# Sums of squares of the last layer's head norms: one four-pass product against two one-pass products of a high and a low part

## The reference

```python
def rms_norm_2(x, g):
    xf = x.astype(jnp.float32)
    y = xf * lax.rsqrt(jnp.mean(xf * xf, axis=-1, keepdims=True) + EPS)
    return (y * g.astype(jnp.float32)).astype(x.dtype)

k = rms_norm_2(k.reshape(B, T, B_HEADS, HEAD_DIM), k_gain)
q = rms_norm_2((h @ w_q).reshape(B, T, B_HEADS, HEAD_DIM), q_gain)
...
decay = c[:, :, q0:q1, None] - c[:, :, None, :q1]
s = jnp.where(causal, s + decay, -jnp.inf)
p = jax.nn.softmax(s, axis=-1)
```

## Time and profile before

| what | value |
|---|---|
| runs, median of 3 (lowest to highest) | 1271.04 us (1270.38 to 1271.95) |
| the profiled execution's own time | 1271.81 us |
| its span from first to last instruction | 1269.8 us |
| mean granted TensorE clock | 0.997 |
| share of the span with an instruction: TensorE matmuls, weight loads | 98%, 92% |
| VectorE, ScalarE, GpSimd | 64%, 58%, 29% |
| instructions | 26957 |
| transfers | 218.68 MB, mean 172 GB/s |

### The profile page before, as it was taken

One profiled execution on the slowest core, in us unless ns is written; L12 is line 12 of the kernel. 1 busy time (PEld: TensorE's weight loads), 2 busy tenths in 40 slices (PEclk: granted clock), 3 DMA queues, 4 the chain that ended last, 5 costly groups with the idle time before them and its releaser, 6 DMA issues.

```text
span 1269.8 us, 26957 instructions
## 1 busy us (share of the span) xinstructions
PE 1245.5 (98%) x9610; PEld 1173.9 (92%) x9610; DVE 812.0 (64%) x1441; ACT 734.6 (58%) x1368; POOL 365.6 (29%) x413
## 2 busy tenths in 40 slices
PE   6999999999999999999999899999999999999998
PEld 6988999998998999998889599999999889999887
DVE  5687755566677655557799975554547766755554
ACT  6476766655455566666566864444346776544433
POOL 2011344421000144441133037770001210678100
PEclk9999999999999999999999899999999999999999
DMA  7542666667665466667655056556555443665764
GB/s 262 182 125 85 195 186 181 185 212 203 206 188 167 135 186 183 193 182 217 183 163 153 6 165 184 178 175 184 172 166 194 146 135 105 194 182 183 199 188 159
DMA packets 65761, 218.68 MB, mean 172 GB/s; under 512 B 9152, under 2 KB 13456, under 8 KB 65552
## 3 DMA queue, kind: packets, MB, share of 16 engines
q1 hardware_dynamic: 63344, 210.99, 54.9%
q10 hardware_dynamic: 2336, 6.58, 1.6%
HBM read 214.04 MB, written 1.08 MB: 169 GB/s over the span
## 4 chain that ended last, share of the span: by engine, by line
PE 76%; issue 10%; DVE 5%; POOL 4%; ACT 3%; DMA 1%; POOLq 0%; SPq 0%; ACTq 0%; DVEq 0%
PE bank L346 19%; PE bank L348 18%; PE bank L347 18%; PE bank L362 8%; PE bank L363 4%; POOL scratch L613 1%; DVE wlo L330 1%; POOL scratch L611 1%; PE bank L960 1%; PE bank L945 1%; POOL ahi_alo L615 1%; PE bank L942 1%; DVE scratch L601 1%; ACT ahi_alo L586 1%; ACT whi L325 1%
## 5 line engine op out<-in xcount | busy, mean ns | idle before, releaser
L330 DVE TENSOR_TENSOR wlo<-raw,whi 128x1024 fp32r<-128x1024 f32 (+1 forms) x391 | 479.7, 1228 | 150.1 <-ACT whi L325 148.3
L346 PE MATMUL bank<-uhi,whi 128*128 128x256 f32 (+1 forms) x1824 | 525.6, 288 | 11.5 <-DVE wlo L330 10.6
L348 PE MATMUL bank<-uhi,wlo 128*128 128x256 f32 (+1 forms) x1824 | 518.0, 284 | 0.0
L347 PE MATMUL bank<-ulo,whi 128*128 128x256 f32 (+1 forms) x1824 | 517.5, 284 | 0.0
L325 ACT ACTIVATE whi<-raw 128x1024 fp32r<-128x1024 f32 (+1 forms) x391 | 407.7, 1045 | 178.6 <-PE bank L363 102.8
L346 PEld LDWEIGHTS bank<-uhi,whi 128*128 128x128 f32 x1824 | 345.4, 189 | 19.8 <-issue 17.1
L348 PEld LDWEIGHTS bank<-uhi,wlo 128*128 128x128 f32 x1824 | 345.6, 189 | 0.0
L347 PEld LDWEIGHTS bank<-ulo,whi 128*128 128x128 f32 x1824 | 344.2, 189 | 0.5
L362 PE MATMUL bank<-ahi_alo,whi 128*128 128x512 f32 x608 | 212.4, 393 | 0.0
L363 PE MATMUL bank<-ahi_alo,wlo 128*128 128x256 f32 x608 | 170.5, 280 | 0.0
L346 PE MATMUL bank<-ahi_alo,whi 128*128 128x272 f32 (+1 forms) x560 | 162.6, 290 | 0.4 <-DVE wlo L330 0.4
(11 more groups left out here) (292 smaller groups left out, 1332.5 us busy)
## 6 DMA issues: line engine op xcount, KB each, us to landing
raw<-stream SPq DMA_DIRECT2D x391, 512.0 KB, 3.9
scratch<-decay ACTq DMA_DIRECT2D x8, 416.0 KB, 4.3
scratch<-relh ACTq DMA_DIRECT2D x8, 384.0 KB, 3.5
scratch<-scratch SPq DMA_DIRECT2D x60, 34.0 KB, 2.6
constants<-consts SPq DMA_DIRECT2D x1, 1300.0 KB, 11.0
h<-xT SPq DMA_DIRECT2D x4, 256.0 KB, 5.4
out<-h SPq DMA_DIRECT2D x8, 128.0 KB, 2.4
scratch<-scratch SPq DMA_DIRECT2D x16, 16.0 KB, 3.2
```

Source lines behind the costliest of these rows:

```text
L330: dve.tensor_tensor(wlo[:, s, 0:w], raw[:, s, 0:w], whi[:, s, 0:w].bitcast(F32), ALU.subtract).then_inc(w_lo, 1)
L346: pe.matmul(dst, hi, a, start=first and i == 0, stop=False)
L347: pe.matmul(dst, hi, b, start=False, stop=False)
L348: mm = pe.matmul(dst, lo, a, start=False, stop=last and i == chunks - 1)
```

## The change

The squares are kept as two parts in the one-pass type: a high part, which ScalarE's Square writes directly into the (here unused) chunks 16 and 17 of the split buffer `ahi`, and a low part, which GpSimd computes as the full square minus the high part and writes to `alo`. TensorE makes two one-pass matmuls per block, with a copy of `headones` in the one-pass type (`sums_r`, made once on ScalarE), in place of one four-pass matmul.

For odd blocks ScalarE writes the full square too, as a second Square; for even blocks GpSimd computes it as a product. The stat of the even block moves from between the scores and unit(2s+1) to inside that unit, after five of its eight chunks. GpSimd's additions for pair s+1 come behind the low parts of blocks 2s and 2s+1. VectorE's evictions wait for the low part instead of the Square before they reuse a buffer.

```diff
--- before.py
+++ after.py
@@ -305,6 +305,7 @@
         ki_copied, wi_scaled, wi_turned, wi_done, ix_ready, ix_relu, ix_acc, ix_mask, ix_clear = sems(
             "ki_copied wi_scaled wi_turned wi_done ix_ready ix_relu ix_acc ix_mask ix_clear")
         h_half = sem("h_half")
+        fox_sq_k, fox_sq_q, fox_lo = sems("fox_sq_k fox_sq_q fox_lo")
         f_exp, f_log = sems("f_exp f_log")
         q_tables, q_neg, q_eps = sems("q_tables q_neg q_eps")
         t_q, t_gather, t_s, t_row, t_max, t_exp, t_p, t_pt, t_pts, t_o, t_ohi, t_olo = sems(
@@ -1164,6 +1165,35 @@
             return j if j < 2 else j + 1
 
         FOX_V = {5: 2, 6: 17, 7: 18}
+        sums_r = ahi[:, 20, 0:P]
+
+        def fox_square(j):
+            return (x[:, 16 + j % 2, fox_cols(j)] for x in (ahi, alo))
+
+        def fox_low_pool(pool, j):
+
+            cols, i, r0 = fox_cols(j), fox_at(j), RFIRST["fkq"]
+            hi, lo = fox_square(j)
+            if j % 2:
+                pool.wait_ge(fox_sq_q, j // 2 + 1)
+            else:
+                y = yb[:, i % 4, cols]
+                pool.wait_ge(evac, BSTART["fkq"] + i + 1)
+                pool.tensor_tensor(ysq[:, 0, cols], y, y, ALU.mult).then_inc(fox_sq_k, 1)
+                pool.wait_ge(fox_sq_k, j // 2 + 1)
+            pool.wait_ge(y_sq, r0 + j + 1)
+            pool.tensor_tensor(lo, ysq[:, j % 2, cols], hi.bitcast(F32), ALU.subtract).then_inc(fox_lo, 1)
+
+        def fox_pool(pool):
+            for j in (0, 1):
+                fox_low_pool(pool, j)
+            for s in (0, 1):
+                decay_pool(pool, s)
+            for s in range(1, fox.pairs):
+                for j in (2 * s, 2 * s + 1):
+                    fox_low_pool(pool, j)
+                if s + 1 < fox.pairs:
+                    decay_pool(pool, s + 1)
 
         def fox_pe(pe):
             a, n0, b0, r0, v0, last = fox, START["fkq"], BSTART["fkq"], RFIRST["fkq"], VFIRST["fv"], fox.pairs - 1
@@ -1190,9 +1220,11 @@
 
             def stat(j):
                 cols = fox_cols(j)
-                pe.wait_ge(y_sq, r0 + j + 1)
-                pe.matmul(block_bank(fox_at(j))[:, 0:width(cols)], const("headones"), ysq[:, j % 2, cols],
-                          start=True, stop=True).then_inc(y_stat, 1)
+                pe.wait_ge(fox_lo, j + 1)
+                hi, lo = fox_square(j)
+                dst = block_bank(fox_at(j))[:, 0:width(cols)]
+                pe.matmul(dst, sums_r, hi, start=True, stop=False)
+                pe.matmul(dst, sums_r, lo, start=False, stop=True).then_inc(y_stat, 1)
 
             def last_early_turn():
                 v = LATE["fv"] - 1
@@ -1228,8 +1260,7 @@
                 else:
                     late_turn(5)
                 scores(s - 1)
-                stat(2 * s)
-                unit(2 * s + 1)
+                unit(2 * s + 1, inside=lambda s=s: stat(2 * s))
                 if s >= 2:
                     values(s - 2)
             values_unit(6, 2 * last + 1, inside=lambda: stat(2 * last + 1))
@@ -1256,7 +1287,14 @@
                 cols, i = fox_cols(j), fox_at(j)
                 act.wait_ge(evac, b0 + i + 1)
                 act.wait_ge(y_stat, r0 + j - 1)
-                act.activation(ysq[:, j % 2, cols], yb[:, i % 4, cols], ACT.Square).then_inc(y_sq, 1)
+                if j == 0:
+                    act.activation(sums_r, const("headones"), ACT.Copy).then_inc(link.sem, 1)
+                    act.wait_ge(link.sem, link.next())
+                act.activation(ahi[:, 16 + j % 2, cols], yb[:, i % 4, cols], ACT.Square).then_inc(y_sq, 1)
+                if j % 2:
+                    if j > 1:
+                        act.wait_ge(fox_lo, j - 1)
+                    act.activation(ysq[:, 1, cols], yb[:, i % 4, cols], ACT.Square).then_inc(fox_sq_q, 1)
 
             def rms(j):
                 cols = fox_cols(j)
@@ -1330,7 +1368,7 @@
                 cols, i = fox_cols(j), fox_at(j)
                 dve.wait_ge(w_used, n0 + i + 1)
                 if j >= 3:
-                    dve.wait_ge(y_sq, r0 + j - 3 if j > 4 else r0 + 2)
+                    dve.wait_ge(fox_lo, j - 3 if j > 4 else 2)
                 if j in (2, 5):
                     dve.wait_ge(v_turned, VFIRST["fv"] + (5 if j == 2 else 6))
                 dve.tensor_tensor(yb[:, i % 4, cols], bank[2 + (b0 + i) % 2][:, 0:width(cols)], rstd[:, 0, cols],
@@ -2552,8 +2590,7 @@
             pool.memset(area(V0, 8 * 384).rearrange("p (c n) -> p c n", n=384)[:, :, 256:384], 0.0).then_inc(v_cleared, 1)
             sqrelu_pool(pool, "up2", WHOLE, 2 * FC1, 0)
             norm_pool(pool, 6, WHOLE)
-            for s in range(fox.pairs):
-                decay_pool(pool, s)
+            fox_pool(pool)
             norm_pool(pool, 7, FIRST)
             sqrelu_pool(pool, "up3", FIRST, 2 * FC1 + FC2, FC2)
```

## The result

| | before | after |
|---|---|---|
| median of 5 runs (lowest to highest) | 1271.04 us (1270.18 to 1272.27) | 1277.87 us (1276.91 to 1279.15) |
| ratio, 95% interval | | 1.0051 (1.0039 to 1.0063) |
| the profiled execution's own time, its span | 1271.81, 1269.8 us | 1279.15, 1277.2 us |
| mean granted TensorE clock | 0.997 | 0.997 |

The change costs 6.8 us (5.0 to 8.0 by the interval). 1277.7 was predicted, inside 1273.6 to 1281.5.

A forecast was written before the change was run, and what follows sets the result against it. A ScalarE and VectorE chain was taken as the bound from the third pair: start +2.65, six rounds of 11.33 instead of 10.59 make +7.1, less 0.2 twice, +6.7. On the median 1277.7 us, range 1273.6 to 1281.5.

The forecast's parts named there:

- The round closes through ScalarE and VectorE, with TensorE in it nowhere: One pair of heads, 10.59 us between odd stats: a ScalarE and VectorE chain bounds it from the third pair on.
- X: End of VectorE's even (key) block eviction in a round; E+3.74 before, predicted E+4.48.
- Cheaper sum product: Two one-pass matmuls per stat save TensorE 0.16 to 0.2 us; only Ln's earlier start, 0.60 instead of 0.80, counts.
- E: End of VectorE's odd (query) block eviction, from which times in a round are counted; next one predicted at X+6.85.
- The second path: ScalarE's second Square delays the weight split 0.33 us; low split ends E+2.98, before the stat path's E+3.22, adding nothing.
- Port collision: GpSimd's additions slow VectorE's low split and norm product through shared SBUF ports; 0.10 us a round reaches X.
- leg T: Not in the prediction: way from odd stat through TensorE's scores, VectorE's maximum and softmax Exp to the next E.
- The start: First blocks, before steady rounds: low parts wait behind GpSimd's eight additions and a low split; stat 3 late by 2.65 us.
- TensorE is the bound: Rival: the odd stat is covered and TensorE's savings count; -4.5, 1266.5 us; chance 0.07.
- the full collision: Rival: the odd subtract waits out VectorE's low split, 1.2 us in each of six rounds; 1285 us; chance 0.12, partial included.
- Only the split path counts: Rival: only the held-back weight split costs, 0.33 us a round; 1274 us, or 1273 with start covered; chance 0.18 together.
- Rival 4: Additions spill past X, removing the even stat's 0.7 us cover; up to 0.5 us a round, 1280.5; 0.63 with forecast.

The follow-up runs named there:

- before_reorder: Kernel before the change, with VectorE evicting the even block before making the attention output's low part; 1270.39 us, 0.9993, and 0.9988 when timed again.
- after_reorder: Changed kernel, with VectorE evicting the even block before making the attention output's low part; 1277.89 us, 1.0057 against the kernel before.
- decay_later: Changed kernel, with GpSimd's causal additions moved behind the next even block's low part; 1277.05 us, 1.0044 against the kernel before.
- square_twice: Changed kernel, with odd blocks back on the four-pass product, plus a second ScalarE Square that nobody reads; 1274.49 us, 1.0027 against the kernel before.
- odd_vector: Changed kernel, with VectorE making the odd block's square and low part, replacing ScalarE's second Square and GpSimd's subtract; 1275.15 us, 1.0030 against the kernel before.

## Why the prediction was right, and where it was lucky

Step by step, in its order:

- **The round closes through ScalarE and VectorE, with TensorE in it nowhere.** Right for the kernel before: before_reorder moved X by 0.34 us and the round followed by 0.21. For the kernel after this is the step that failed. The change put the stat so late that the way through TensorE's scores became the longer one. after_reorder shows it: X 0.33 us earlier, the round still 11.28.
- **Cheaper sum product.** A pair is 0.13 us apart without a wait (1030.38 to 1030.51) and 0.22 behind one (1024.95 to 1025.17), as derived. It was worth nothing that I can find except for Ln, which starts at S+0.54 (0.60 predicted, 0.80 before), and 0.2 us at the very end.
- **Even stat moved.** No wait in a steady round, as predicted. The low part was ready at 1029.25 = X+1.57 (1.8 predicted), and TensorE came to the stat at X+2.70 (2.3 or later), 1.1 us behind it. At the start two even stats waited, stat 0 as well as stat 2, so TensorE waited for GpSimd 10 times where 7 to 9 were predicted.
- **Odd stat.** Second Square at E+0.35, subtract at E+0.83 for 0.73, stat at E+1.61 (1.67 predicted), TensorE's stall 1.06 (1.1). The norm product began at E+3.11 (3.22).
- **The second path adds nothing more.** Right in the sum: the low split ran from E+1.73, as forecast, and ended at 1026.39, just before the norm product started at 1026.45. Its stand-alone price of 0.33 a round measured 0.31.
- **Port collision, 0.10.** Right in kind and size, wrong in effect. Low split 1.32 us instead of 1.23, norm product 0.55 instead of 0.48, and both are back to normal where the additions move (X - E 4.28 instead of 4.34 in decay_later). The split's 0.09 was hidden behind the stat path, the norm product's 0.07 was not. So the collision cost X 0.06 us, and the round nothing, since leg T was longer. The Trainium skill, "SBUF — State Buffer", section "SBUF: two separate sides", says that the loser blocks for a whole instruction. The rows agree in kind: the four additions took 2.87 us here and 1.72 in decay_later. But the side that lost was mostly GpSimd's (1.15 us, against 0.16 us of VectorE's), so the 1.8 us that the prediction worked out from the page did not come.
- **A round, 11.33.** Measured 11.28. My 6.85 + 4.48 had X 0.14 us too late, and X to E measured 6.94 instead of 6.85, which is leg T at work. Two small errors of opposite sign stood on top of a leg that is 0.09 us shorter than the binding one. The size was right because both legs pass through the same late stat. Leg T, worked out from the kernel before with the odd stat at its predicted place, is 1.67 + 4.56 - 0.17 (the cheaper sum product) + 5.27 = 11.33, the same number, so the time of a round could not tell the two apart.
- **The start, +2.65 at stat 3.** Measured +2.33. Stat 0 is late by 0.67 (0.68 predicted) and stat 1 by 1.01. The odd subtract behind it did meet a low split, as forecast, and took 1.08 us, 0.35 more (0.3 predicted). Stat 2 came at 14.98 (15.27 predicted), but "a microsecond after TensorE comes to it" was wrong: TensorE came 0.2 to 0.4 us before it. decay_later says why the mistake hurt nothing: TensorE's own arrival, at 14.60, is 3.2 us later than in the kernel before, and I had charged GpSimd with a delay that TensorE mostly had anyway from the stat's new place and the late blocks before it. The start also moves by some tenths between executions with the landing of the first decay transfer (after_reorder), so its 0.3 us of error is within that.
- **The sum.** +6.7 predicted; +6.28 from entry to end, +6.8 between the medians. The rounds gave 4.14 (4.44 predicted), the start 2.33 (2.65), and 0.20 came back (0.4). That 1277.7 met the median of 1277.87 within 0.2 us is luck: the stage was forecast 0.4 us too long, and the interval of the ratio is 3 us wide. "Nothing later takes it back" holds: from stat 15 to the end it is 218.57 us before and 218.37 after.

Of the rivals, "TensorE is the bound" would have given odd stats under 10.5 apart, the full collision 12.5; neither came in the steady rounds (at stat 3 alone, part of the collision did). "Only the split path counts" is what square_twice does, and it measured 1274.49 where the rival said 1274, so its price was right and only its condition did not hold. Rival 4 did not come either, but it was near: the additions ended at 1027.73, X+0.05, and GpSimd began the even square at X+0.08; the even Ln started without a wait for its stat.

## What to carry to other kernels

- A cheaper instruction on an engine that waits is worth nothing; what counts is when its inputs are ready. Here TensorE saved 1.9 us in all and stood still for 1.06 us in every round.
- An engine with idle time still has a place in a semaphore chain. Ask of each added instruction which instruction stands behind it on its engine, and of each hand-over between engines how much later its receiver starts: 0.31 us a round for a Square that nobody read, 1.1 us for a Square, a hand-over and a subtract.
- When a periodic round is laid out, look for every place where two waits join and give each leg its length. One leg found to match the round does not show that it binds in the changed kernel; an edit that moves one leg alone does.

## What the runs showed of the hardware that I had not expected

- GpSimd's product of a tile with itself took 0.64 us for 128 x 272 (L1182), against 0.77 for the subtract of two tiles of the same size (L1185) right behind it. The number of operands, the operation and the output type all differ, so which of these it is stays open.
- VectorE's eviction, which reads one operand from a PSUM bank, took its usual 0.42 us at 1020.92 in odd_vector while GpSimd's additions were under way; the two instructions behind it, with their operands in SBUF, took 0.65 and 0.56 instead of 0.42.
- A stall of 1.06 us each 11.28 us left TensorE's granted clock alone: it read 1.00 from 971 to 1065 us, its level of 2.4 GHz, in the kernel after as in the one before.
